# Differential attention: squares turned by TensorE and added up by VectorE, two casts moved to ScalarE

## What is computed

```python
def differential_attention(q, k, v, lam):
    # q,k: (B,H,2,S,Dh), v: (B,H,S,2Dh)
    s = einsum('bhcqd,bhckd->bhcqk', q, k) * scale          # causal
    p = softmax(where(causal, s, -inf), axis=-1)
    a = p[:, :, 0] - lam * p[:, :, 1]
    return einsum('bhqk,bhke->bhqe', a, v)

def diff_layer(x, k, v, ...):
    q, gate = split(rms_norm(x, norm_g) @ w_in, 2)
    q = apply_rope(rms_norm(q, q_norm_g), cos, sin)         # mean of squares over 64
    o = rms_norm(differential_attention(q, k, v, lam), subln_g) * (1 - lam_init)  # over 128
    return (silu(gate) * o) @ w_out
```

## Time and profile before

| what | value |
|---|---|
| median of 3 runs | 647.96 us (647.7 to 650.9) |
| the profiled execution | 647.47 us, its span 646.2 us |
| TensorE busy | 623.3 us (96%) |
| VectorE, ScalarE, GpSimd busy | 448.2, 334.4 and 352.2 us |
| TensorE clock granted | 1.00 of full speed in all stretches looked at |

### The profile page before, as it was taken

The page is one execution under the profiler, slowest core; times in us unless marked ns, Lnnn a source line. Parts: engine busy times, 40 slices in busy tenths (PEclk is TensorE's granted clock), DMA queues, the critical chain, the costliest instruction groups (busy, mean ns, idle before and its releaser), DMA issues.

```text
span 646.2 us, 9996 instructions
## 1 busy us (share of the span) xinstructions
PE 623.3 (96%) x3324; PEld 525.6 (81%) x3324; DVE 448.2 (69%) x701; ACT 334.4 (52%) x728; POOL 352.2 (54%) x339
## 2 busy tenths in 40 slices
PE   5999999999999999999998999999899999999998
PEld 4788778888888888888887888788688888887786
DVE  3486177979788797983327298605779999998541
ACT  5342184676747667584316625424456645576320
POOL 5556396546565555743541454447575775556161
DMA  7433122112131220211211322222322220221142
GB/s 260 107 101 98 50 83 81 49 50 65 37 91 38 62 65 32 81 51 53 67 61 34 106 95 93 81 82 67 102 78 66 81 76 13 74 83 66 32 135 93
DMA packets 61774, 49.08 MB, mean 76 GB/s; under 512 B 7729, under 2 KB 48817, under 8 KB 61745
## 3 DMA queue, kind: packets, MB, share of 16 engines
q1 hardware_dynamic: 58064, 48.25, 24.3%
q10 hardware_dynamic: 3680, 0.46, 0.5%
HBM read 44.50 MB, written 2.10 MB: 72 GB/s over the span
## 4 chain that ended last, share of the span: by engine, by line
PE 65%; DVE 20%; ACT 8%; issue 4%; DMA 1%; SPq 0%; DVEq 0%; POOL 0%; ACTq 0%
PE bank L593 17%; PE bank L595 16%; PE bank L594 16%; PE bank L707 6%; ACT pr L1318 4%; PE bank L721 3%; PE bank L692 3%; DVE hi L1483 2%; DVE small L1680 2%; DVE pr L1701 1%; DVE at_lo L1735 1%; DVE h_hi L1446 1%; DVE v L1398 1%; DVE lo L1488 1%; DVE qs L1629 1%
## 5 line engine op out<-in xcount | busy, mean ns | idle before, releaser
L471 POOL TENSOR_TENSOR w_lo<-w_raw,w_hi 128x512 fp32r<-128x512 f32 x60 | 82.2, 1377 | 120.4 <-ACT w_hi L1015 120.4
L483 POOL TENSOR_TENSOR w_lo<-w_raw,w_hi 128x512 fp32r<-128x512 f32 x100 | 143.3, 1433 | 8.0
L481 POOL CAST w_hi<-w_raw 128x512 fp32r<-128x512 f32 x100 | 75.7, 757 | 129.5 <-DVE pr L1701 35.7
L593 PE MATMUL bank<-h_hi,w_hi 128*128 128x512 f32 x320 | 129.3, 404 | 2.1 <-ACT q L1227 2.0
L593 PE MATMUL bank<-w_hi,h_hi 128*128 128x512 f32 x320 | 128.3, 401 | 2.9 <-DVE h_lo L1404 2.8
L595 PE MATMUL bank<-w_hi,h_lo 128*128 128x512 f32 x320 | 125.7, 393 | 0.0
L594 PE MATMUL bank<-w_lo,h_hi 128*128 128x512 f32 x320 | 125.6, 392 | 0.0
L595 PE MATMUL bank<-h_hi,w_lo 128*128 128x512 f32 x320 | 125.4, 392 | 0.0
L594 PE MATMUL bank<-h_lo,w_hi 128*128 128x512 f32 x320 | 125.1, 391 | 0.0
L593 PEld LDWEIGHTS bank<-w_hi,h_hi 128*128 128x128 f32 x320 | 60.7, 190 | 16.0 <-DVE h_lo L1404 3.5
L593 PEld LDWEIGHTS bank<-h_hi,w_hi 128*128 128x128 f32 x320 | 60.1, 188 | 16.5 <-ACT q L1227 1.9
(11 more groups left out here) (174 smaller groups left out, 1194.6 us busy)
## 6 DMA issues: line engine op xcount, KB each, us to landing
w_raw<-in_a_w_in SPq DMA_DIRECT2D x64, 256.0 KB, 2.7
w_raw<-in_w_kv SPq DMA_DIRECT2D x32, 256.0 KB, 3.1
w_raw<-in_b_w_in SPq DMA_DIRECT2D x32, 256.0 KB, 2.8
w_raw<-in_a_w_out SPq DMA_DIRECT2D x16, 256.0 KB, 2.7
w_raw<-in_b_w_out SPq DMA_DIRECT2D x16, 256.0 KB, 3.0
xs<-in_x SPq DMA_DIRECT2D x4, 512.0 KB, 4.8
qrot<-qs SPq DMA_DIRECT2D x32, 64.0 KB, 2.0
out_x<-xs SPq DMA_DIRECT2D x8, 256.0 KB, 2.6
```

The costliest lines, as they stand in the source:

```text
L471: nc.gpsimd.tensor_tensor(w_lo[s][:, :], w_raw[s][:, :], w_hi[s][:, :].bitcast(F32), ALU.subtract).then_inc(s_w, 1)
L481: nc.gpsimd.tensor_copy(w_hi[s][:, :], w_raw[s][:, :]).then_inc(s_whi, 1)
L483: nc.gpsimd.tensor_tensor(w_lo[s][:, :], w_raw[s][:, :], w_hi[s][:, :].bitcast(F32), ALU.subtract).then_inc(s_w, 1)
L593: pe.matmul(o, ahi, bhi, start=start, stop=False, skip_group_check=True)
```

## The change

Four things in the head loop:

1. In heads 0 to 6 TensorE transposes the squares (four blocks of `qsq` into bank 1, four of `osq` into bank 3, `turned_squares`) where it multiplied them by ones. VectorE adds them up with one or two reductions over 128 x 512 in PSUM (`turned_means`) and then adds epsilon in one or two small instructions. The transposes wait for the combined probabilities (`s_cm`); the next head's masks wait until VectorE has read the banks (`s_rq`). Head 7 and the end keep the old sums.
2. The cast of the gated output (`keep_hi`) moves from VectorE to ScalarE in heads 2 to 7.
3. The casts of two of the four slabs of each head move from GpSimd to ScalarE, between ScalarE's square of the output and its copies `at_hi`. GpSimd's subtraction then waits for ScalarE (`s_whia`).
4. Order: on ScalarE the root stands behind `at_hi`, and `q_copy` ahead of the gate's exponential in heads 1 to 5; on VectorE the Newton steps stand behind `at_lo`, and in head 0 `q_rotate(2)` ahead of the first combination.

```diff
 ACT_HI = [*(v_slab(n) for n in range(RING_A, 16)), *range(G_OUT + RING_A, G_OUT + 16),
-          *(kv_slab(n) for n in range(RING_B, 32)), *range(H_OUT + RING_B, H_OUT + 16)]
+          *(kv_slab(n) for n in range(RING_B, 32)),
+          *(H_BODY + 4 * h + n for h in range(1, 8) for n in (0, 1)), *range(H_OUT + RING_B, H_OUT + 16)]
...
             if g in ACT_HI:
-                pool.wait_ge(s_whia, ACT_HI.index(g) + 1)
+                pool.wait_ge(s_whia, i * 2 + (ACT_HI.index(g) + 1))
                 nc.gpsimd.tensor_tensor(w_lo[s][:, :], w_raw[s][:, :], w_hi[s][:, :].bitcast(F32),
...
             nc.gpsimd.tensor_copy(w_hi[s][:, :], w_raw[s][:, :]).then_inc(s_whi, 1)
-            pool.wait_ge(s_whi, i * per + (g + 1 - sum(a < g for a in ACT_HI)))
+            pool.wait_ge(s_whi, i * (2 if per == 4 else per) + (g + 1 - sum(a < g for a in ACT_HI)))
             nc.gpsimd.tensor_tensor(w_lo[s][:, :], w_raw[s][:, :], w_hi[s][:, :].bitcast(F32),
...
+        def turned_squares(h, o):
+
+            pe.wait_ge(s_cm, h + 1)
+            pe.wait_ge(s_qq, h + 2)
+            for i in range(TT):
+                tr = pe.transpose(bank[1][:, cols(i * P, P)], qsq[:, cols(i * P, P)], ident[:, :])
+            if o is not None:
+                pe.wait_ge(s_oq, o + 1)
+                for i in range(TT):
+                    tr = pe.transpose(bank[3][:, cols(i * P, P)], osq[:, cols(i * P, P)], ident[:, :])
+            tr.then_inc(s_sum, 1)
+
         turn_after = {12: 0, 13: 1, 15: 2, 16: 3, 20: 4, 21: 5, 22: 6, 24: 7}
...
             pe.wait_ge(s_v, KT + 1 if first else h * 2 + KT)
+            if not first:
+                pe.wait_ge(s_rq, h + (R_HEAD - 1))
             for c in (1, 0):
...
             def sum_and_turn():
-                sums(h + 1, h - 1 if n_before else None)
+                turned_squares(h, h - 1 if n_before else None)
                 turn_probs(h)
...
         def sum_and_turn_last():
-            sums(h + 1, h - 1)
+            turned_squares(h, h - 1)
             turn_probs(h)
...
-        def slab_hi(g):
+        def slab_hi(g, i=0, per=0):
             s = slot_of(g)
-            act.wait_ge(s_wl[s], 16 * loads_of(g))
-            act.wait_ge(s_wu, g - ring(g) + 1)
+            act.wait_ge(s_wl[s], (i * 16 if per else 0) + 16 * loads_of(g))
+            act.wait_ge(s_wu, i * per + (g - ring(g) + 1))
             A(w_hi[s][:, :], w_raw[s][:, :], ACT.Copy).then_inc(s_whia, 1)
...
-        def head(h, first=False, gate=None, q_used=None, q_next=True, later=None):
+        def head(h, first=False, gate=None, q_used=None, q_next=True, later=None, slabs=None, keep=True):
             if gate is not None:
...
                 if b == 1 and gate is not None:
+                    if q_used is not None:
+                        q_copy(h + 3, q_used)
                     gate_exp(h + KT)
...
                     q_square(2)
-            if q_used is not None:
-                q_copy(h + 3, q_used)
+            if q_used is not None and first:
+                q_copy(3, q_used)
             if later is not None and h == KT - 2:
...
                 output_square(h - 1)
+            if keep:
+                act.wait_ge(s_og, h + (KT - 1))
+                A(h2_hi[:, bass.ds(h - 2, 1), :].rearrange("p a n -> p (a n)"), og[:, :], ACT.Copy).then_inc(s_oh, 1)
             if later is not None and h == KT - 1:
                 gate_exp(h + KT + 1)
-            c0, c1 = mean_cols(first, not q_next)
-            root(means[:, c0:c1], means[:, 12 + c0:12 + c1], R_HEAD, h, 1)
+            if slabs is not None:
+                slab_hi(H_BODY + 4, *slabs)
+                slab_hi(H_BODY + 5, *slabs)
             for b in range(3):
...
                 A(at_hi[:, cols(*BANKS[b])], bank[BANK_B[0, b]][:, 0:BANKS[b][1]], ACT.Copy).then_inc(s_ah, 1)
+            c0, c1 = mean_cols(first, not q_next)
+            root(means[:, c0:c1], means[:, 12 + c0:12 + c1], R_HEAD, h, 1)
         def output_square(h, o=bank[7]):
...
-        head(0, first=True, q_used=H_BODY + 2)
-        with act.Fori(1, KT - 2) as i:
-            head(i, gate=i * 4 + H_BODY, q_used=i * 4 + (H_BODY + 2))
-        head(KT - 2, gate=H_GATES, later=H_GATES + 2)
+        head(0, first=True, q_used=H_BODY + 2, slabs=(0, 4), keep=False)
+        head(1, gate=H_BODY + 4, q_used=H_BODY + 6, slabs=(1, 4), keep=False)
+        with act.Fori(2, KT - 2) as i:
+            head(i, gate=i * 4 + H_BODY, q_used=i * 4 + (H_BODY + 2), slabs=(i, 4))
+        head(KT - 2, gate=H_GATES, later=H_GATES + 2, slabs=(KT - 2, 4))
         head(KT - 1, q_next=False, later=H_GATES + 4)
...
+        def turned_means(with_o):
+
+            st.link(V.tensor_reduce(means[:, 0:8], comps(bank[1][:, :]), AX.X, ALU.add))
+            if with_o:
+                st.link(V.tensor_reduce(means[:, 8:12], bank[3].rearrange("p (t d) -> p t d", d=P), AX.X, ALU.add))
+            ins = TS(means[:, 0:8], means[:, 0:8], DH * EPS, None, ALU.add)
+            if with_o:
+                ins = STT(out=means[:, 8:12], in0=means[:, 8:12], scalar=1.0 / P, op0=ALU.mult, in1=eps_sums,
+                          op1=ALU.add)
+            ins.then_inc(s_rq, 1)
+
         def root_newton(c0, c1, n):
...
+            if not n_before:
+                q_rotate(2)
             combine((3, 2), 2, 4)
...
                 gate_silu(h + KT)
-            if not n_before:
-                q_rotate(2)
-            elif q_next:
+            if q_next and n_before:
                 q_add(h + 2)
...
             if n_before == 2:
-                keep_hi(h - 2, h + (KT - 1))
                 keep_lo(h - 2, h + (KT - 1))
...
             dve.wait_ge(s_sum, h + 2)
-            mean_squares(c0, c1)
-            root_newton(c0, c1, h + R_HEAD).then_inc(s_rb, 1)
-            st.link(STT(out=eps_sums, in0=tiny[:, 16:24:2], scalar=EPS, op0=ALU.mult, in1=tiny[:, 16:24:2],
-                        op1=ALU.mult))
+            if q_next:
+                turned_means(n_before)
+            else:
+                mean_squares(c0, c1)
             for b in range(3):
...
                     at_hi[:, cols(*BANKS[b])].bitcast(F32), ALU.subtract).then_inc(s_al, 1)
+            root_newton(c0, c1, h + R_HEAD).then_inc(s_rb, 1)
+            st.link(STT(out=eps_sums, in0=tiny[:, 16:24:2], scalar=EPS, op0=ALU.mult, in1=tiny[:, 16:24:2],
+                        op1=ALU.mult))
             if q_after:
...
         with dve.Fori(2, KT - 2) as i:
-            st.enter(i, 2, 10)
+            st.enter(i, 2, 12)
             head(i, 2)
```

## The result

The changed kernel takes 651.92 us (median of 20 runs, 650.1 to 652.67) where the kernel before takes 648.07 us: the ratio is 1.0054, 95% interval 1.0042 to 1.0065. By the ratio it is slower by 3.5 us, against a forecast of 2.8; the time forecast was 650.8 us. The profiled execution took 652.12 us, with a span of 650.9 us.

The account below looks back on a forecast made before the run. VectorE's closed chain was taken to bound the loop, with TensorE as a limit from below. Heads 0, 1, 2 to 5 and 6 gave -2.2 + 1.0 + 2.4 + 1.6 = +2.8 us, so 650.8 us median, range 644.0 to 654.5.

Parts of the forecast that it names:

- head 0: First head: early rotation ends VectorE's idle 2.29 us for qrot; between -1.0 and -2.9 us, taken as -2.2.
- VectorE as the bound, TensorE's saving at nothing: Loop heads: VectorE runs a closed chain, so TensorE's 0.86 us less per head is hidden and counts for nothing.
- three signs: Wrong if reductions are not near 0.69 us, TensorE's clock falls below 1.00 in new gaps, or loop period stays below 19.9.
- 275 ns: TensorE: skill's time per 128x128 transpose; eight would be 2.2 us, 0.5 more than the sums; set aside for 0.105 us each.
- The loop head: Heads 2 to 5: each changes by between -0.7 and +1.1 us, taken as +0.6; four heads +2.4 us.
- The walk: Head 4's instructions followed in its old times, with the same waits: next maxima at 548.5, 0.2 us earlier than before.
- The full stop: Loop head: a Newton step or small row on VectorE meets a GpSimd subtraction and costs up to 1.07 us more.
- The quarter: Loop head: a quarter of the 1.07 us stop given back, since `qc` comes later against the subtraction it waited for.
- The reductions: VectorE, loop head: two added reductions of 128x512 from PSUM, nearest row 0.684 us, with links 1.46 us together.
- B: Rival, slower: loop heads +1.1 us each from full stops and ScalarE's lateness; +6.2 us in all, 654.2 us; chance 0.17.
- the ring: Slower rival's mechanism in loop heads: ScalarE's slab casts through GpSimd's subtraction to VectorE's small steps, +1.1 us each.
- A's limit: Faster rival (643.5 us, chance 0.2): TensorE never waits, -5.6 - 3.4 = -9.0, giving 639 us at best.

Follow-up runs that it names:

- old sums: The changed kernel with the sums of squares back on TensorE, multiplied by ones, all else kept: 652.95 us, ratio 1.0082 to the kernel before.
- small values in PSUM: The changed kernel, complete, with sums, means and Newton middle values of heads 0 to 6 in free bank 7 columns: 640.66 us, ratio 0.9878 to before.
- old root: The changed kernel with the root ahead of `at_hi` on ScalarE and Newton steps ahead of `at_lo` on VectorE: 662.87 us, ratio 1.0237 to before.

## Why the prediction was right

Head by head, from maxima to maxima in the two traces (measured, and in brackets forecast): head 0 -2.10 us (-2.2), head 1 +1.04 (+1.0), heads 2 to 5 together +3.31 (+2.4), head 6 +1.77 (+1.6), the rest behind head 7's maxima -0.08 (0). That is +3.9 us, against +2.8 forecast; most of the difference is in the loop. The traces differ by 0.76 us more ahead of head 0, where the code is the same; in the other traces head 0 begins anywhere from 446.1 to 448.9 us, so that belongs to the executions.

- **VectorE as the bound, TensorE's saving at nothing.** Right: eight transposes took 0.93 us (0.84 forecast), TensorE was busy for 1.4 us less of the 20 us window, and it waited for `og` instead. One of the three signs that it gave for being wrong did appear, in head 7 alone: the clock fell to 0.50 behind the wait for `og`, grown from 1.11 to 3.40 us. The time behind head 7's maxima is no longer for it (-0.08 us).
- **The 275 ns of the Trainium skill** ("TensorE: Matmul & The Clock Gate", Part 4: PE-mode transpose) are the length of one transpose, and the trace agrees: 272 ns. The prediction set them against the 0.105 us from one transpose to the next, and multiplied them by eight; since the transposes overlap, eight took 0.93 us, and neither number contradicts the other.

```profile
L827 PE MATMUL bank<-ident,osq x24: 272/272/273, 479.2 to 583.0; 128*128 128x128 f32 x24
```

- **The loop head, mis-sized.** +0.6 was forecast and +0.83 measured. The walk had GpSimd start 0.3 us later than before; it did. It had `h_lo` stopped until about 541.7 in head 4's old times; `h_lo` came ahead of the subtraction (which had been issued at 540.82 behind `q_lo`), took 0.69 us, and the stop fell on the epsilon step instead (1.06 us). The full stop on a small row came as priced (1.26 us against 0.17). The quarter that was to be given back by `qc` was not: it still took 1.78 us, and `qs` grew from 0.68 to 0.96. That is the term that was wrong. Summed up, `at_lo` began 14.03 us behind the maxima (14.38 in the walk, 16.05 before), and from there to the next maxima it took 6.69 us (6.12 in the forecast, 3.85 before). The time is thus near by two errors of opposite sign, -0.35 and +0.57 us.
- **Head 0.** -2.10 us against -2.2 is in part luck. The wait of 2.29 us for `qrot` is gone, as forecast. In its place VectorE waits 2.19 us for ScalarE's copy of q, ahead of the early rotation, and small steps take 1.06 and 1.22 us; neither is in the prediction.
- **The reductions.** Their length was right (0.69 us), their price as a term of its own was not: taken out, they return 0.17 us in heads 2 to 4 and 2 us in each of heads 5 and 6. A sum of lengths does not describe this stage.
- **The lock of the Trainium skill** ("SBUF — State Buffer", "Who interferes with whom") agrees in all points that were tested: small rows between SBUF and SBUF end with GpSimd's instruction, reductions keep 0.69 us. With one operand in PSUM the small rows keep 0.17 to 0.18 us.
- **What the prediction undervalued.** It treated the order of root and Newton steps, and the two slab casts, as neutral. They are worth about 11 and 4 us. The first has a mechanism that it did not name: a late `at_lo` stops TensorE, and in most heads 1.2 GHz follow.
- **The rivals.** B, with ScalarE's casts as the head of the ring, is refuted as a cause, since undoing them costs 4 us; as a size it was about as near as the forecast (loop 20.72 us, between 20.5 and 21.0). The chances were 0.44 for a time up to 651.2 us and 0.38 for more; 651.92 is just past that line. A's limit was read wrongly. The 3.4 us taken for all of TensorE's waits are two of five rows; the view also has 1.1 us for `og`, 0.5 for `ot` and 0.4 for `at_lo`, 5.4 us in all. With them the limit is -11.0 us, 637, and not 639. The best complete kernel here took 640.66 us.

What stays open is how the kernel with the old sums divides its loss between the clock and the port. Its heads alternate between 19.63 and 21.57 us, and the shorter one holds the stretch of 1.2 GHz. No run separates them.

## What to carry to other kernels

Before moving work between VectorE and GpSimd, list for each instruction whether it works between SBUF and SBUF. In these traces those, the reductions apart, are the ones that stood still for GpSimd, whatever their size, and a chain of tiny ones was the worst. Putting the tiny values into spare PSUM columns was worth 11 us where moving 1.5 us of real work about was worth little. A saving on the busiest engine is worth measuring by its bound (narrow the competitor's work and read the period), since it can be real and hidden: undoing a part that looks harmful may be slower still.

## What was not expected of the hardware

- VectorE instructions of 12 columns with one operand in PSUM took 0.17 to 0.18 us in the middle of GpSimd's subtractions. Between SBUF and SBUF, instructions of 4 to 12 columns took up to 1.26 us.
- TensorE's clock went from 2.4 to 1.2 GHz for about 3.5 us behind a wait of only 0.50 us followed by sixteen matmuls of one or two columns (old sums, head 4). It did the same behind the wait of 3.40 us in the changed kernel, behind one of 1.78 us in head 7 with small values in PSUM, and for about 6 us behind one of 2.76 us (old root, head 5). It stayed at 2.4 GHz behind waits of 1.57 us in the changed kernel and 2.15 us (old root, head 1), and behind 0.60 us with the same sixteen narrow matmuls (old sums, head 1). The length of the wait alone does not sort these cases, and no run here separates what does.
